# One-hot matmuls of a dense expert pass: pieces of 8 tokens in bf16, weights split into three parts on VectorE

## What is computed

```
u = peer_u[idx]
a = gelu(einsum('cd,chkd->chk', xc, u))
v = peer_v[idx]
out = einsum('chk,chkd->cd', g * a, v)      # g: softmax of the 16 scores of a head
```

## Time and profile before

| | |
|---|---|
| median of 3 runs | 3508.41 us (3502.19 to 3519.32) |
| span of the profiled execution | 3496.3 us, 12.1 us below the median |
| PE busy | 3015.2 us, 86% |
| DVE busy | 2640.8 us, 76% |
| ACT busy | 833.1 us, 24% |
| POOL busy | 2267.8 us, 65% |
| moved by DMA | 1261.58 MB, mean 361 GB/s |

### The profile page before, as it was taken

One profiled execution on the slowest core, in us unless ns is written; L12 is line 12 of the kernel. 1 busy time (PEld: TensorE's weight loads), 2 busy tenths in 40 slices (PEclk: granted clock), 3 DMA queues, 4 the chain that ended last, 5 costly groups with the idle time before them and its releaser, 6 DMA issues.

```text
span 3496.3 us, 32133 instructions
## 1 busy us (share of the span) xinstructions
PE 3015.2 (86%) x8978; PEld 1535.9 (44%) x8978; DVE 2640.8 (76%) x6158; ACT 833.1 (24%) x2063; POOL 2267.8 (65%) x1942
## 2 busy tenths in 40 slices
PE   7897798899988898888997996559998899989987
PEld 4665344567554443433443431125543344544332
DVE  2217878797778888878998899889966778875566
ACT  2111232422122332143221121125510014530000
POOL 0005644688556657788886677777776666777775
PEclk9898798878998998989998998779999999989998
DMA  6349987999999999999999999999999999999998
GB/s 158 102 146 368 386 287 242 327 399 383 400 336 381 361 400 356 370 370 353 387 384 395 407 384 374 356 382 409 408 409 409 409 408 409 408 396 409 409 409 346
DMA packets 426294, 1261.58 MB, mean 361 GB/s; under 512 B 61063, under 2 KB 106791, under 8 KB 426106
## 3 DMA queue, kind: packets, MB, share of 16 engines
q0 software_dynamic: 276480, 1006.76, 74.2%
q1 hardware_dynamic: 141701, 247.01, 20.5%
q10 hardware_dynamic: 7936, 5.77, 0.5%
HBM read 1230.09 MB, written 29.29 MB: 360 GB/s over the span
## 4 chain that ended last, share of the span: by engine, by line
PE 37%; DMA 23%; POOL 17%; DVE 12%; issue 8%; SPq 2%; ACT 1%; ACTq 0%; POOLq 0%; DVEq 0%
PE pY L1724 9%; POOL ubuf L980 9%; DMA vbuf<-in_peer_v_dram,idx 9%; POOL vbuf L992 7%; DMA ubuf<-in_peer_u_dram,idx 7%; PE pb L1346 5%; PE pb L1592 4%; DVE ubuf L2408 4%; PE pb L1610 4%; PE pb L1697 3%; PE pb L1638 2%; DMA R<-in_w_in_dram 2%; PE pb L1681 2%; DMA R<-c_scratch 2%; DVE acc L2429 1%
## 5 line engine op out<-in xcount | busy, mean ns | idle before, releaser
L980 POOL DMA_INDIRECT ubuf<-in_peer_u_dram,idx x1088 | 1296.8, 1192 | 842.7 <-DVE idx L2392 293.2
L2408 DVE CUSTOM_DVE_ANT_0 ubuf<-ubuf,hnf 128x1024 f32<-128x1024 f32 x946 | 1141.8, 1221 | 278.7 <-DMA ubuf<-in_peer_u_dram,idx 271.2
L992 POOL DMA_INDIRECT vbuf<-in_peer_v_dram,idx x832 | 967.9, 1163 | 371.5 <-issue 219.5
L1724 PE MATMUL pY<-vbuf,dg 128*128 128x512 f32 (+1 forms) x1952 | 1012.2, 650 | 217.5 <-DMA vbuf<-in_peer_v_dram,idx 174.1
L1724 PEld LDWEIGHTS pY<-vbuf,dg 128*128 128x128 f32 (+1 forms) x1952 | 358.2, 197 | 680.7 <-issue 407.5
L2429 DVE SCALAR_TENSOR_TENSOR acc<-vbuf,gw,acc 128x1024 f32<-128x1024 f32 x344 | 441.8, 1284 | 78.7 <-DMA vbuf<-in_peer_v_dram,idx 72.7
L1697 PE MATMUL pb<-R 128*128 128x512 f32 x1024 | 457.8, 596 | 0.4 <-DMA R<-in_peer_v_dram 0.4
L1592 PE MATMUL pb<-R 128*128 128x256 f32 (+2 forms) x1152 | 360.1, 473 | 9.0 <-DMA R<-in_w_in_dram 6.3
L1697 PEld LDWEIGHTS pb<-R 128*128 128x128 f32 x1024 | 197.3, 193 | 250.0 <-issue 248.8
L1592 PEld LDWEIGHTS pb<-R 128*128 128x128 f32 x1152 | 221.2, 193 | 145.6 <-issue 92.8
L1638 PE MATMUL pb<-R 128*128 128x256 f32 (+2 forms) x768 | 250.5, 482 | 9.2 <-DMA R<-in_w_query_dram 8.4
(11 more groups left out here) (260 smaller groups left out, 2653.0 us busy)
## 6 DMA issues: line engine op xcount, KB each, us to landing
R<-in_peer_v_dram SPq DMA_DIRECT2D x128, 512.0 KB, 6.8
R<-in_w_in_dram SPq DMA_DIRECT2D x12, 2048.0 KB, 20.2
R<-in_w_in_dram SPq DMA_DIRECT2D x24, 1024.0 KB, 12.2
R<-in_w_query_dram SPq DMA_DIRECT2D x24, 1024.0 KB, 17.0
ubuf<-in_peer_u_dram,idx POOLq DMA_INDIRECT x1088, 10.3
vbuf<-in_peer_v_dram,idx POOLq DMA_INDIRECT x832, 11.4
R<-in_w_out_dram SPq DMA_DIRECT2D x12, 1024.0 KB, 9.2
R<-in_x_prompt_dram SPq DMA_DIRECT2D x16, 512.0 KB, 10.2
```

The costliest lines, as they stand in the source:

```text
L980: pool.indirect_dma_start(out=ubuf[:, n % RING, :], out_offset=None, in_=peer_u[0], in_offset=bass.IndirectOffsetOnAxis(ap=idx[:, t % NI, ...
L992: pool.indirect_dma_start(out=vbuf[:, v % RING, :], out_offset=None, in_=peer_v[0], in_offset=bass.IndirectOffsetOnAxis(ap=idx[:, t % NI, ...
L1724: ins = pe.matmul(pY[0:rows, half, :], dg[:, CPE[m] % RDG, 0:rows], vbuf[:, v % RING, half * 512:(half + 1) * 512], start=first, stop=(t ! ...
L2408: dve.tensor_tensor_reduce(ubuf[:, n % RING, :], ubuf[:, n % RING, :], hn, 1.0, 0.0, ALU.mult, ALU.add, dots[:, q % 2, n % GRP:n % GRP + 1 ...
```

## The change

Pieces have 8 tokens (`NTOK`), so a half has 32. `oh` makes three things in bf16 on DVE: B, A, and B times the weight, where the weight is split into three bf16 parts that sum up to it (`d_sp` makes them, `oh_w` holds the three products). The tokens are the innermost dimension, so DVE reads and writes runs of 8, and a matmul's neighbouring columns lie 8 elements apart. `ow` is gone. `wm` does three bf16 matmuls per token that accumulate in PSUM. The pieces alternate between PSUM banks 4 and 0 (`WBANK`), and `we` copies each piece of 512 columns. As bank 0 is one of those in which `dm` accumulates, the first `wm` of half 1 waits for both `dy` of half 0. The one-hot ring has 2 buffers of 8 tokens, before 3 of 4. An iota in bf16, repeated 8 times, is made once in `mixw`; `dT` moves into `gf`. The planner's costs of these stages are changed.

```diff
-    NTOK = 4
+    NTOK = 8
     NPIECE = 2 * P // NTOK
-    NEV = NPIECE // 2
-    OHR, VRR = 3, 3
+    OHR, VRR = 2, 3
+    WBANK = (4, 0)
...
+            put(j + 3, "d_sp", ps, j)
-        at = 3
+        at = 4
         for half in range(2):
             for p in range(NPIECE):
                 put(at + p, "oh", ps, half, p)
-                put(at + p, "ow", ps, half, p)
                 put(at + p + 1, "wm", ps, half, p)
-                if p % 2:
-                    put(at + p + 1, "we", ps, half, p // 2)
+                put(at + p + 1, "we", ps, half, p)
...
-            return {"dm": 3.2, "wm": 1.2, "d_T": 0.7}[stage], 0
-        if stage in ("oh", "dy", "d_ab"):
-            return 0, {"oh": 2.2, "dy": 1.3, "d_ab": 0.9}[stage]
+            return {"dm": 3.2, "wm": 2.4, "d_T": 0.7}[stage], 0
+        if stage in ("oh", "dy", "d_ab", "d_sp"):
+            return 0, {"oh": 5.8, "dy": 1.3, "d_ab": 1.5, "d_sp": 0.9}[stage]
...
                 def wm(ps, half, p):
                     o = (2 * ps + half) * NPIECE + p
-                    pe.wait_ge(ow_d, o + 1)
-                    if p % 2 == 0:
-                        pe.wait_ge(we_d, NT_D + o // 2)
+                    pe.wait_ge(oh_d, NT_D + o + 1)
+                    if o >= 2:
+                        pe.wait_ge(we_d, NT_D + o - 1)
+                    if half and p == 0:
+                        pe.wait_ge(dy_d, 2)
                     for a in range(NTOK):
-                        c = (p % 2 * NTOK + a) * NB
-                        ins = pe.matmul(pb[:, 4, c:c + NB], oh_a[o % OHR][:, a, :], oh_b[o % OHR][:, a, :],
-                                        start=True, stop=True)
+                        for x in range(3):
+                            ins = pe.matmul(pb[:, WBANK[o % 2], a * NB:(a + 1) * NB], oh_a[o % OHR][:, :, a],
+                                            oh_w[o % OHR][:, x, :, a], start=(x == 0), stop=(x == 2))
...
+                        dve.tensor_copy(iota8, iota[:].unsqueeze(2).to_broadcast([P, NK, NTOK]))
...
+                def d_sp(ps, j):
+                    dve.wait_ge(we_d, 2 * ps + j + 1)
+                    step(dve.tensor_tensor(w_rest, pb[:, WBANK[j], 2 * P:3 * P], dT[:, j, 2, :], ALU.subtract))
+                    step(dve.tensor_copy(dT[:, j, 3, :], w_rest))
+                    step(dve.tensor_tensor(dT[:, j, 4, :], w_rest, dT[:, j, 3, :], ALU.subtract))
...
                 def oh(ps, half, p):
-                    dve.tensor_tensor(oh_a[o % OHR], iota[:].unsqueeze(1).to_broadcast(shape),
-                                      dT[:, j, 0, t0:t0 + NTOK].unsqueeze(2).to_broadcast(shape), ALU.is_equal)
-                    shape = [P, NTOK, NB]
-                    dve.tensor_tensor(oh_b[o % OHR], iota[:, half * NB:(half + 1) * NB].unsqueeze(1).to_broadcast(shape),
-                                      dT[:, j, 1, t0:t0 + NTOK].unsqueeze(2).to_broadcast(shape), ALU.is_equal
-                                      ).then_inc(oh_d, 1)
+                    shape = [P, NB, NTOK]
+                    steps[0] += 1
+                    dve.tensor_tensor(oh_b[o % OHR], iota8[:, half * NB:(half + 1) * NB, :],
+                                      dT[:, j, 1, tok].unsqueeze(1).to_broadcast(shape), ALU.is_equal).then_inc(dve_s, 1)
+                    shape = [P, NK, NTOK]
+                    dve.tensor_tensor(oh_a[o % OHR], iota8, dT[:, j, 0, tok].unsqueeze(1).to_broadcast(shape), ALU.is_equal)
+                    dve.wait_ge(dve_s, steps[0])
+                    shape = [P, 3, NB, NTOK]
+                    dve.tensor_tensor(oh_w[o % OHR], oh_b[o % OHR].unsqueeze(1).to_broadcast(shape),
+                                      dT[:, j, 2:5, tok].unsqueeze(2).to_broadcast(shape), ALU.mult).then_inc(oh_d, 1)
```

More of the change, by code:

```diff
@@ L180, in build @@
     NB = NK // 2
-    NTOK = 4
+    NTOK = 8
     NPIECE = 2 * P // NTOK
-    NEV = NPIECE // 2
-    OHR, VRR = 3, 3
+    OHR, VRR = 2, 3
+    WBANK = (4, 0)
+    assert NPIECE % 2 == 0 and NTOK * NB == 512
     NT_D = 2 * len(PASSES)
@@ L830, in build @@
         DO0 = DV0 + VRR * D
-        OHN = NTOK * (NK + NB)
-        oh_a = [R[:, DO0 + k * OHN:DO0 + k * OHN + NTOK * NK].rearrange("p (t a) -> p t a", t=NTOK) for k in range(OHR)]
-        oh_b = [R[:, DO0 + k * OHN + NTOK * NK:DO0 + (k + 1) * OHN].rearrange("p (t b) -> p t b", t=NTOK)
+        OHN = NTOK * (NK + 3 * NB) // 2
+        oh_a = [R[:, DO0 + k * OHN:DO0 + k * OHN + NTOK * NK // 2].bitcast(BF16).rearrange("p (a t) -> p a t", t=NTOK)
                 for k in range(OHR)]
-        DT0 = DO0 + OHR * OHN
-        dT = R[:, DT0:DT0 + 6 * P].rearrange("p (j x t) -> p j x t", j=2, x=3)
-        assert DT0 + 6 * P <= 22592
+        oh_w = [R[:, DO0 + k * OHN + NTOK * NK // 2:DO0 + (k + 1) * OHN].bitcast(BF16).rearrange(
+            "p (x b t) -> p x b t", x=3, t=NTOK) for k in range(OHR)]
+        OB0 = DO0 + OHR * OHN
+        oh_b = [R[:, OB0 + k * NB * NTOK // 2:OB0 + (k + 1) * NB * NTOK // 2].bitcast(BF16).rearrange(
+            "p (b t) -> p b t", t=NTOK) for k in range(OHR)]
+        assert OB0 + OHR * NB * NTOK // 2 <= 22592
+        gf16 = gf[:].bitcast(BF16)
+        dT = gf16[:, 0:10 * P].rearrange("p (j x t) -> p j x t", j=2, x=5)
+        w_rest = gf[:, 5 * P:6 * P]
+        iota8 = mixw[:].rearrange("p g c -> p (g c)").bitcast(BF16)[:, 0:NK * NTOK].rearrange("p (a t) -> p a t", t=NTOK)
         ab_f = [R[:, DO0 + j * OHN:DO0 + j * OHN + 2 * P].rearrange("p (x k) -> p x k", x=2) for j in range(2)]
@@ L912, in build @@
         y_out = [sem("y_out0"), sem("y_out1")]
-        oh_d, ow_d, wm_d, we_d, dm_d, dy_d = (sem(x) for x in ("oh_d", "ow_d", "wm_d", "we_d", "dm_d", "dy_d"))
+        oh_d, wm_d, we_d, dm_d, dy_d = (sem(x) for x in ("oh_d", "wm_d", "we_d", "dm_d", "dy_d"))
         HN_COPIED = [PH * GN + 1, PH * GN + 2]
@@ L1692, in dm @@
                             pe.wait_ge(dy_d, 2)
-                        pe.wait_ge(we_d, NT_D + NEV * (2 * ps + half + 1))
+                        pe.wait_ge(we_d, NT_D + NPIECE * (2 * ps + half + 1))
                     pe.wait_ge(wu_in[u % VRR], vr_in(u))
@@ L1955, in d_cp @@
                     act.wait_ge(wm_d, k + 1)
[L1956 to L1966, removed]
+                    act.activation(dT[:, j, 0:3].rearrange("p x t -> p (x t)"), pb[:, WBANK[j], 0:3 * P], ACT.Copy
+                                   ).then_inc(we_d, 1)
                 def we(ps, half, e):
-                    o = (2 * ps + half) * NEV + e
-                    act.wait_ge(wm_d, NT_D + 2 * o + 2)
+                    o = (2 * ps + half) * NPIECE + e
+                    act.wait_ge(wm_d, NT_D + o + 1)
                     if o == 0:
@@ L1975, in we @@
                         act.wait_ge(dm_d, NB * (2 * ps + half))
-                    j, t0 = e // (NEV // 2), e % (NEV // 2) * 2 * NTOK
-                    act.activation(dw[j][:, :, t0:t0 + 2 * NTOK], pb[:, 4, :].rearrange("p (t b) -> p b t", b=NB),
+                    j, t0 = divmod(e * NTOK, P)
+                    act.activation(dw[j][:, :, t0:t0 + NTOK], pb[:, WBANK[o % 2], :].rearrange("p (t b) -> p b t", b=NB),
                                    ACT.Copy).then_inc(we_d, 1)
@@ L2014, in _ @@
                          "kt_cp": kt_cp, "o_cp": o_cp, "s_ex": s_ex, "sig": sig, "h_sq": h_sq, "h_sd": h_sd, "hT_cp": hT_cp,
-                         "q_cp": q_cp, "q_load": q_load, "s_cp": s_cp, "gexp": gexp, "d_cp": d_cp, "ow": ow,
+                         "q_cp": q_cp, "q_load": q_load, "s_cp": s_cp, "gexp": gexp, "d_cp": d_cp,
                          "we": we}, picks)
@@ L2460, in oh @@
                     j, t0 = divmod(p * NTOK, P)
-                    if p == 0 and half == 0:
-                        dve.wait_ge(we_d, NT_D)
+                    tok = slice(t0, t0 + NTOK)
                     if o >= OHR:
                         dve.wait_ge(wm_d, NT_D + o - OHR + 1)
-                    shape = [P, NTOK, NK]
-                    dve.tensor_tensor(oh_a[o % OHR], iota[:].unsqueeze(1).to_broadcast(shape),
-                                      dT[:, j, 0, t0:t0 + NTOK].unsqueeze(2).to_broadcast(shape), ALU.is_equal)
-                    shape = [P, NTOK, NB]
-                    dve.tensor_tensor(oh_b[o % OHR], iota[:, half * NB:(half + 1) * NB].unsqueeze(1).to_broadcast(shape),
-                                      dT[:, j, 1, t0:t0 + NTOK].unsqueeze(2).to_broadcast(shape), ALU.is_equal
-                                      ).then_inc(oh_d, 1)
+                    shape = [P, NB, NTOK]
[8 more added lines that the diff above has]
+                                      dT[:, j, 2:5, tok].unsqueeze(2).to_broadcast(shape), ALU.mult).then_inc(oh_d, 1)
                 def dy(half, j):
```

6 lines of the change are left out of this document (2 added, 4 removed).

## The result

The changed kernel takes 3574.41 us (median of 4 runs, 3569.49 to 3576.7), the kernel before 3508.02 beside it (4 runs): ratio 1.0181, 95% interval 1.0158 to 1.0204. It is 66 us slower; 3513 was forecast, with 3497 to 3550 as the range. The profiled span is 3572.1 us.

What follows compares the result with a forecast made beforehand. DMA's ceiling of 408 to 409 GB/s was taken to bound both buildings. POOL 1 (half 0) + 4 (half 1) + 2 (dy wait) - 2 (ACT's departure) = +5 us on 3508.4, giving 3513; range 3497 to 3550.

Steps and rivals of the forecast that it cites:

- The moving side doesn't matter … so the load sets the pace: PE's weight-building matmuls: the stationary load sets a pass's price, 0.05 to 0.07 us, so 1.2 to 1.7 us per 8 tokens.
- The dear bound: Upper bound on a bf16 pass in PE's weight building: 0.124 us and above.
- PE's part of the sum: PE's cheaper weight-building passes: worth nothing in the total, DMA being full.
- Rival A: PE becomes the bound in the buildings: 0.124 us a pass gives +32 us, 3540; 0.2 gives 3656; chance 0.12.
- Rival C: PE, with less to do, is granted the lower clock more often in the building: +15 us, 3523; chance 0.05.
- 4 us of backlog: Building of half 0: gathers land in 10.2 us against 6.1 with a short queue, covering delays before DMA idles.
- The wait for dy: Start of half 1: PE stands some 8 us for both dy; 0 to 7 us lost, 2 taken.
- POOL: Gathers delayed by longer DVE instructions: +5 us of POOL per half, counted as 1 in half 0 and 4 in half 1.
- the ceiling: DMA moves at most 408 to 409 GB/s in building and multiplying alike; at most 2.7 us to be won.
- ACT's 135 us: ACT's L1965 work over both halves falls away; it gives only a shorter chain and counts in the 2.7 us.
- rival B: DVE falls to one element a cycle in the one-hot instructions: 3564; chance 0.08.
- Rival D: The change is faster, needing a bound other than DMA in the buildings: 3502; chance 0.08.

Runs made afterwards that it cites:

- mov_flat: Changed kernel with the weight matmuls' moving operand read from adjacent columns, products wrong: 3592.16 us on the chip of 3597.93; repeated as mov_flat_again, 3516.59 on that of 3507.15.
- stride2: Changed kernel with 2 tokens innermost instead of 8, columns 4 bytes apart: 3588.47 us on the chip of 3597.93; repeated as stride2_again, 3518.90 on that of 3507.15.
- stride2_no_dy: Changed kernel with 2 tokens innermost and half 1 on bank 4 alone, so without the wait for both dy: 3514.55 us, ratio 1.0004 to the kernel before.
- stride4: Changed kernel with 4 tokens innermost instead of 8, columns 8 bytes apart: 3519.38 us, ratio 1.0032 to the kernel before.

## Why the prediction was wrong

**The step that failed: "The moving side doesn't matter … so the load sets the pace", and from it 0.05 to 0.07 us a pass.** It was read off rows whose operands are contiguous. With columns 16 bytes apart the moving side sets the pace: 0.121 us for 64 columns, against 0.060 with the moving operand contiguous. The stationary operand's load is in the shadow of that, 146 ns in place of the 98 of the earlier trace rows. The dear bound, "0.124 and above", was on record, and the value was at it: PE's part of the sum was put at nothing, and it was most of the loss.

The Trainium skill's rule in "SBUF — State Buffer", section "Specifications (TRN2)", which the prediction set against the change and did not follow, is right in direction here: the price rises as fewer columns share a 16-byte line. Its figure of two hits for full bandwidth isn't borne out: at 8 bytes, two columns to a line, a pass takes 0.061 us against 0.035 at 4 bytes, with both operands at that distance.

**Rival A was the mechanism, its price too low: 3540.** Half 0, added up from PE's timelines: each group from its start to the next start, idle time taken off.

| us | before | after |
|---|---|---|
| `wm` | 59.5 | 93.0 |
| weighing (316 and 324 passes) | 143.5 | 158.5 |
| L1657, after L1663 | 3.1 | 3.7 |
| idle | 8.4 | 0.9 |
| sum | 214.5 | 256.1 |

So the +41 are 33.5 for `wm` and 15 for the weighing, less 7.5 of idle time used up. Two picks more account for 3.4 us of the weighing (8 passes at 0.43, as 5.33 less 3.61 us are four of them). **About 13 us are the clock**: a mean of 0.92 means that 16% of 256 us, 41, ran at half speed, which loses at most 20.5; before it was 0.97 and some 7. Ten weighings that take 1.7 us longer show 17 of the 20. A had 32 - 14 - 4 = +14, to be held against the 30 us of DMA time lost (11 of the 41 us went with 4.5 MB more moved):
- it took a run of 8 passes of before at 0.99 us, from L1565. In this stage they take 0.84, 0.105 a pass (first two rows below), so a piece costs 1.22 us more and not 1.0: 7 us a half;
- it counted 14 us of idle time. There were 8.4; the sum of counts and prices left out what the stretch of the earlier trace rows, PE busy in 77.82 of 80 us, said directly;
- it had no clock. Rival C had it alone and for another reason, less work. On the second and third chip it falls in the kernels whose pieces take 2.76 or 2.90 us and PE never pauses (0.95 and 0.93 from 2440 us on), and stays at 1.00 there with the same instructions in 1.43, 1.47 or 0.84 us. On the first chip it falls with cheap pieces too (0.94 in mov_flat, 0.89 in stride2, from 2440 to 2600 us), where PE stops within pieces. That the dear passes bring the clock down is read from this association; no run changed the clock alone;
- its 4 us of backlog, subtracted, were there: a gather takes 6.1 us to land in the changed kernel from 2440 to 2600 us, before 10.3 in the same window.

```profile
2440.98 1.00 PE L1681 MATMUL pb<-R 128*128 128x64 f32 x8
2441.82 3.65 PE L1724 MATMUL pY<-vbuf,dg 128*128 128x512 f32 x8
...
2330.38 1.97 PE L1681 MATMUL pb<-R 128*128 128x64 f32 x8 [5.74 <-ACT R L1965]
...
2344.66 3.12 PE L1687 MATMUL pb<-R 128*128 128x64 bf16 x24 [10.80 <-DVE R L2477]
```

The last two rows, of the kernel before and of the changed one, are the first pieces, both at a granted clock of 0.50. The contiguous passes take 1.97 us in place of 1.00; the dear ones 3.12 in place of 3.08. So what sets the price of a dear pass isn't PE's clock.

In half 1 A was too low too: +18 forecast, 35 us of DMA time lost. The building is 16 us longer: 28 for `wm`, 8 for the weighing, less 20 of idle time (21.3 before, 1.5 after); the mean clock is 0.90, before 0.94. The wait for dy, ahead of it, comes on top.

**The wait for dy: 2 us forecast, 7 to 8 measured.** PE stood 11.9 us instead of 8, as the two `dy` are 8.4 us apart (4.3 before). The 7 to 8 are against the same kernel without the wait; against the kernel before, the same stretch is only 1 to 2 us longer in stride2_again.

**Not forecast: the start.** From the first step to the first `wm` it takes 15 to 16 us instead of 7 to 9: the first product now stands behind `d_sp` and three one-hot steps (PE waits 10.8 us for L2477). On the two later chips every kernel of the new structure has 13 to 16 us here, whatever its passes cost, so 4 to 9 us go to the steps added ahead of the stage; no run takes them away alone.

**POOL: +5 us per half forecast, nothing found in the sum.** From the first `wm` to the first `dm` of half 0, 162 gathers keep POOL busy 166.5 us before (second profile) and 165.3 us in stride2_no_dy. The mechanism is there: counted in these traces, 46 gathers of before and 44 of stride2_no_dy start inside a one-hot instruction, and of the 76 with more than 0.13 us of it left 73 take the rest plus 0.81 us, to a few ns. They average 1.18 and 1.22 us against 0.94, which costs 11 and 12 us, where the forecast's random starts give 10 and 15. So it was worth 1 or 2 us, not 5. The other gathers were as much shorter, 0.970 and 0.955 us; why was not looked into.

**Right:** the ceiling. ACT's 135 us, DVE's time and PE's, when it was made cheap, bought nothing. The three DVE instructions take 424, 686 and 952 ns, forecast 425, 717 and about 1010, so rival B was out. Rival D found nothing to gain. With passes as cheap as taken the change costs 9 to 12 us by the medians (mov_flat_again 3517, stride2_again and stride4 3519, before 3507), and stride2_no_dy 5 or 6 (3515, before 3509; by its ratio 1). That the sum, +5, comes near is partly luck: its POOL term was too high and the start was missing.

## What to carry to other kernels

A layout that suits one engine is paid by the next reader: put the innermost dimension where DVE has its short runs of 2 elements and TensorE its columns 4 bytes apart, and both were satisfied here. If no row of a trace has the access pattern that an edit introduces, the dear bound is as good a candidate as the cheap one: measure one group first. An engine that is busy 97% of a stretch has next to no room, whatever a sum of counts and prices leaves over. And the price of what an edit replaces is read in its own stage, not from the nearest look-alike.

## What the hardware showed that I had not expected

- A pass of 128 stationary and 64 moving bf16 columns, from start to start: 0.035 us with columns 4 bytes apart, 0.061 at 8, 0.121 at 16; 0.060 with stationary 16 and moving contiguous; 0.115 the other way round.
- A dear pass hardly feels the clock: a piece at 0.50 takes 3.12 us, at 1.00 3.08, while the contiguous f32 passes before go from 1.00 to 1.97 us.
- PE's granted clock went to 0.50 for some 3.4 us at a time while its record has no idle time, in stretches with pieces of 2.90 us, in half 0 of the changed kernel always right behind a piece.
- A gather that starts inside a one-hot instruction of DVE takes the rest of that instruction plus 0.81 us, within a few ns, in 73 of 76 cases.
- The same kernel, the one before, takes 3507 to 3509 us on two chips and 3598 on a third, 2.5% more. In the version profiled on both, stride2, DMA moves 355 GB/s there in this stage in place of 406, and PE stops without a visible cause.
